# Second-layer keys kept on the chip, two weight buffers in the front, a first selection that begins with single heads

## The reference, cut to what matters

```python
sh1, sc1, g1, sh2, sc2, g2 = split(silu(c) @ ada_w[l] + ada_b[l])
x = x + g1 * mixer(rms_norm(x) * (1 + sc1) + sh1)
x = x + g2 * peer_ffn(rms_norm(x) * (1 + sc2) + sh2)

def peer_ffn(h):                                  # per block of 128 tokens
    q = (h @ wq).reshape(n, 8, 2, 128)            # 8 heads, two sides
    s = einsum('nhpd,hpkd->nhpk', q, keys)        # 128 keys for each head and side
    v1, i1 = top_k(s[:, :, 0], 16); v2, i2 = top_k(s[:, :, 1], 16)
    top_s, pos = top_k(v1[..., :, None] + v2[..., None, :], 16)   # of 256 pairs
    idx = i1 * 128 + i2 at pos; g = softmax(top_s)
    act = gelu(einsum('nhkd,nd->nhk', w_down[idx], h))
    return einsum('nhk,nhkd->nd', g * act, w_up[idx])
```

## Time and profile before

| | |
|---|---|
| Median of 3 runs | 3246.12 us (3245.19 to 3246.56) |
| The profiled execution | 3249.22 us, span 3247.4 us, mean granted TensorE clock 0.80 |
| Busy | TensorE 2348.6 us (72%), VectorE 2212.8 (68%), ScalarE 1281.3 (39%), GpSimd 1205.5 (37%) |
| Moved | 1288.67 MB, mean 397 GB/s |
| Of it by GpSimd's queue (q0) | 1124.14 MB; by SyncE's (q1) 162.07 MB |
| The chain that ended last | DMA 33%, TensorE 32%, VectorE 20%, ScalarE 8% |

### The profile page before, as it was taken

How to read it: one execution, slowest core, us unless ns; L and a number is a source line. 1 busy time by engine, 2 the same in 40 slices (tenths; PEclk the granted TensorE clock), 3 DMA queues, 4 the chain that set the end, 5 groups by cost and what they waited for, 6 DMA issues and landing times.

```text
span 3247.4 us, 38543 instructions
## 1 busy us (share of the span) xinstructions
PE 2348.6 (72%) x13032; PEld 923.5 (28%) x13032; DVE 2212.8 (68%) x5634; ACT 1281.3 (39%) x3704; POOL 1205.5 (37%) x1076
## 2 busy tenths in 40 slices
PE   6997678576776778786695696956686667856666
PEld 2345234122341235441151261511143112511110
DVE  2314875876569555869858968589948996795444
ACT  2212453345534453533433534333343433443333
POOL 1112243343434342334433434334433453343332
PEclk9998889687887888886696896967687777866676
DMA  8777999999999999999999999999999999999998
GB/s 321 262 284 288 400 377 423 420 395 408 416 422 409 417 398 422 397 422 408 421 402 420 408 413 420 391 403 398 420 398 421 405 421 403 422 398 421 421 420 357
DMA packets 170486, 1288.67 MB, mean 397 GB/s; under 512 B 19632, under 2 KB 20528, under 8 KB 24112
## 3 DMA queue, kind: packets, MB, share of 16 engines
q0 software_dynamic: 154368, 1124.14, 84.9%
q1 hardware_dynamic: 15920, 162.07, 12.0%
HBM read 1284.04 MB, written 2.10 MB: 396 GB/s over the span
## 4 chain that ended last, share of the span: by engine, by line
DMA 33%; PE 32%; DVE 20%; ACT 8%; issue 7%; POOL 1%; DVEq 0%; ACTq 0%; SPq 0%; POOLq 0%
DMA ring<-in_experts,expert 31%; PE psum L1792 10%; DVE ring L1495 8%; PE psum L1559 7%; PE psum L1573 5%; PE psum L1739 3%; DVE arena L1382 3%; PE psum L1531 1%; PE psum L1590 1%; ACT shares_of L1119 1%; ACT diag L1120 1%; PE psum L1545 1%; DVE arena L1410 1%; ACT acts L1118 1%; ACT L1118 1%
## 5 line engine op out<-in xcount | busy, mean ns | idle before, releaser
L1792 PE MATMUL psum<-ring,diag 64*64 64x512 f32 x8192 | 1415.1, 796 | 766.1 <-ACT diag L1120 760.7
L843 POOL DMA_INDIRECT ring<-in_experts,expert x1024 | 1179.8, 1152 | 1791.2 <-PE psum L1792 1654.3
L1495 DVE CUSTOM_DVE_ANT_0 ring<-ring,h 128x1024 f32<-128x1024 f32 x1024 | 1230.8, 1223 | 528.7 <-DMA ring<-in_experts,expert 506.5
L1118 ACT ACTIVATE acts<-dots 128x1 f32<-128x1 f32 x1024 | 206.5, 202 | 1475.2 <-DVE dots L1495 1439.2
L1792 PEld LDWEIGHTS psum<-ring,diag 64*64 64x64 f32 x8192 | 284.1, 161 | 1726.3 <-ACT diag L1120 1536.8
L1120 ACT ACTIVATE diag<-ident_half,shares_of 128x64 f32<-128x64 f32 x1024 | 356.1, 348 | 33.3
L1119 ACT ACTIVATE shares_of<-acts,gate 128x1 f32<-128x1 f32 x1024 | 301.7, 295 | 33.3
L1382 DVE SCALAR_TENSOR_TENSOR arena<-kept,taps,arena 128x128 f32<-128x128 f32 x960 | 262.6, 346 | 0.1
L1573 PEld LDWEIGHTS psum<-arena,weights 128*128 128x128 f32 x1984 | 226.8, 192 | 49.2 <-issue 45.4
L1573 PE MATMUL psum<-arena,weights 128*128 128x128 f32 x1984 | 238.1, 278 | 0.4 <-DMA weights<-in_chunks 0.4
L869 ACT ACTIVATE arena<-psum 128x512 f32<-128x512 f32 (+1 forms) x105 | 65.5, 624 | 219.3 <-PE psum L1573 121.9
(11 more groups left out here) (170 smaller groups left out, 1605.9 us busy)
## 6 DMA issues: line engine op xcount, KB each, us to landing
weights<-in_chunks SPq DMA_DIRECT2D x67, 2048.0 KB
ring<-in_chunks POOLq DMA_DIRECT2D x46, 1024.0 KB, 5.7
ring<-in_experts,expert POOLq DMA_INDIRECT x1024
arena<-in_chunks SPq DMA_DIRECT2D x16, 512.0 KB
ring<-in_chunks SPq DMA_DIRECT2D x3, 2048.0 KB, 8.9
x<-in_x SPq DMA_DIRECT2D x1, 2048.0 KB, 14.0
kept<-in_chunks POOLq DMA_DIRECT2D x2, 1024.0 KB, 18.2
out_x<-x SPq DMA_DIRECT2D x4, 512.0 KB
```

The source lines that it names most:

```text
L843: pool.indirect_dma_start(out=ring[:, k, :], out_offset=None, in_=table, in_offset=bass.IndirectOffsetOnAxis(ap=expert[:, s.b % 2, n:n + 1 ...
L1118: step(act.activation(acts[:, k:k + 1], dots[:, k:k + 1], ACT.Gelu))
L1495: dve.tensor_tensor_reduce(out=ring[:, k, 0:D], in0=ring[:, k, 0:D], in1=h2[:, s.b % 2, :], scale=1.0, scalar=0.0, op0=ALU.mult, op1=ALU.a ...
L1792: pe.matmul(ffn_out[rows_out, r * COLS:(r + 1) * COLS], diag[rows_in, k, :], ring[rows_in, k, D + n * COLS:D + (n + 1) * COLS], start=Fals ...
```

## The change

1. `SIDE` names five buffers instead of three, and the third weight buffer is gone: the chunks of the front have two. GpSimd no longer waits for the last chunk in it.
2. From unit 1 on GpSimd waits for `side_landed[1]` instead of `x_landed`. SyncE's wait for `side_landed[5]` and the first chunk now stand ahead of the eleven small parameter loads.
3. In `FRONT` the values' first phase v0 stands behind w1, t1 and w2 instead of ahead of w1.
4. Selection takes its heads in pieces: `PIECES` as before, `FIRST_PIECES` for block 0 of layer 0, where the first two pieces are one head each. GpSimd may then fetch 16 slots at first, 16 more after the second piece, then 32 each. `SELECT_WITH_EVEN` and `EVEN_LEFT` are written anew for the 28 phases, with 0.7 in place of `SHARED` (0.6).
5. ScalarE's exponential comes ahead of the evacuation of the same phase.
6. The keys' second half in layer 1 has a place of its own (`kept[:, 5120:6144]`). In layer 1 block 0 loads both halves, block 1 the first half only, and blocks 2 and 3 none.

```diff
+PIECES = [(0, 2), (2, 4), (4, 6), (6, 8)]
+FIRST_PIECES = [(0, 1), (1, 2), (2, 4), (4, 6), (6, 8)]
...
-    SIDE = (8, 0, 1)
+    SIDE = (8, 0, 1, 2, 3)
...
-                open_to = range(self.BUFS + (last[c] < gathers[0]))
-                c.buf = min(open_to, key=lambda b: last[held[b]] if held[b] else -1)
+                c.buf = min(range(self.BUFS), key=lambda b: last[held[b]] if held[b] else -1)
...
-        s = Stage("select", layer=layer, b=b, first=first, cost=(1.3,) * (3 if first else 5) + (2.5,) * (5 * QUARTERS))
+        s = Stage("select", layer=layer, b=b, first=first, cost=(1.3,) * (3 if first else 5) + tuple(
+            1.4 if hi - lo == 1 else 2.5 for lo, hi in (FIRST_PIECES if first else PIECES) for _ in range(5)))
...
+            if layer and b > 1 - half:
+                s.keys.append(self.kept_keys[half])
+            else:
+                new.append(self.key((layer * 2048 + half * 1024, layer * 2048 + (half + 1) * 1024),
+                                    s.s[1] if half and not layer else ("ht_ready", s.ht), layer * half))
+                s.keys.append(new[-1])
...
 SELECT_WITH_EVEN = """
-s8 s9 s10 s11 n0 s12 n1 s13 n2 q0 s14 q1 g0 s15 q2 g1 s16 q3 q4 s17 g2 g3 q5 s18 a0 a1 s19 a2 a3 g4 s20 a4 a5 s21 a6 a7 s22
+s8 s9 s10 s11 s12 n0 s13 n1 s14 n2 q0 s15 q1 g0 s16 q2 s17 g1 q3 q4 s18 g2 g3 s19 q5 a0 s20 a1 a2 s21 a3 g4 s22 a4 a5 s23 a6 s24 a7
+s25 a8 a9 s26 a10 a11 s27
 """
...
-q0 u11 q1 t0 k12 w0 v0 w1 t1 q2 q3 q4 v1 w2 r0 q5 a0 w3 a1 ...
+q0 u11 q1 t0 k12 w0 w1 t1 w2 v0 q2 q3 q4 v1 r0 q5 a0 w3 a1 ...
...
-        stages = mixer(1, 3)
-        return alone(p.gate_row(0, G2)) + written(stages | {"s": select}, SELECT_WITH_EVEN, SHARED) + written(stages, EVEN_LEFT)
+        stages = mixer(1, 1)
+        return alone(p.gate_row(0, G2)) + written(stages | {"s": select}, SELECT_WITH_EVEN, 0.7) + written(stages, EVEN_LEFT)
...
-        key_half = at(3072, 1024)
+        keys_at = [at(3072, 1024), kept[:, 5120:6144]]
...
             sp.dma_start(x[:], A["x"].rearrange("(t p) n -> p t n", p=P)).then_inc(x_landed, 16)
+            sp.wait_ge(side_landed[5], 16)
+            load_chunk(0)
             sp.dma_start(iota16[:], A["iota16"]).then_inc(params, 16)
...
-            sp.wait_ge(side_landed[5], 16)
-            for n in range(len(plan.chunks)):
+            for n in range(1, len(plan.chunks)):
                 load_chunk(n)
...
-                    pool.wait_ge(x_landed, 32)
+                    pool.wait_ge(side_landed[1], 16)
...
-            t, part = plan.last_extra.last_use
-            pool.wait_ge(full[t.bank], t.full_after[part])
...
-                    if n % (SLOTS_PER_BLOCK // QUARTERS) == 0:
-                        pool.wait_ge(S["topk_ready"], QUARTERS * s.index + QUARTERS * n // SLOTS_PER_BLOCK + 1)
+                    if n // TOPK in [lo for lo, hi in pieces] and n % TOPK == 0:
+                        chosen_before += 1
+                        pool.wait_ge(S["topk_ready"], chosen_before)
...
-                for n in range(s.lists + 5 * QUARTERS):
+                for n in range(len(s.cost)):
+                    if n >= s.lists and (n - s.lists) % 5 == 4:
+                        exponent((n - s.lists) // 5)
                     what, q, part = s.work[n] if n < len(s.work) else ("wait", 0, 0)
...
-                    if n >= s.lists and (n - s.lists) % 5 == 4:
-                        exponent((n - s.lists) // 5)
                     yield
...
-                for q in range(QUARTERS):
-                    dve.wait_ge(S["scores_ready"], s.sc + q + 1)
-                    lists, heads = range(4 * q, 4 * q + 4), range(2 * q, 2 * q + 2)
+                for i, (lo, hi) in enumerate(s.pieces):
+                    dve.wait_ge(S["scores_ready"], s.sc + lo // 2 + 1)
+                    lists, heads = range(2 * lo, 2 * hi), range(lo, hi)
...
```

More of the change, by code:

```diff
@@ L128, in __init__ @@
         self.turned = None
-        self.keys_loaded = 0
+        self.keys_loaded, self.kept_keys = [0, 0], []
     def tile(self, parts=1):
@@ L135, in chunk, with key @@
         return Chunk(source, cols)
-    def key(self, cols, after):
-        return Chunk(KEY_CH, cols, after)
+    def key(self, cols, after, place):
+        c = Chunk(KEY_CH, cols, after)
+        c.place = place
+        return c
     def place(self):
@@ L153, in place @@
                 last[c] = at
-        gathers = [at for at, (s, phase) in enumerate(self.order) if s.kind == "gather"]
-        held, landed = [None] * (self.BUFS + 1), [0] * (self.BUFS + 1)
+        held, landed = [None] * self.BUFS, [0] * self.BUFS
         for at, (s, phase) in enumerate(self.order):
@@ L373, in select @@
         s.q, s.s = [self.tile() for _ in range(QUARTERS)], [self.tile() for _ in range(QUARTERS)]
-        s.keys = [self.key((layer * 2048 + half * 1024, layer * 2048 + (half + 1) * 1024), s.s[1] if half else ("ht_ready", s.ht))
-                  for half in range(2)]
+        s.keys, new = [], []
+        for half in range(2):
+            if layer and b > 1 - half:
[4 more added lines that the diff above has]
+                s.keys.append(new[-1])
+        self.kept_keys = s.keys
         s.work = SELECT_FIRST if first else SELECT
@@ L383, in select @@
                 s.claim(phase, s.s[q])
-                if q % 2 == 0:
+                if q % 2 == 0 and s.keys[q // 2] in new:
                     s.read(s.keys[q // 2], phase, phase, s.s[q + 1], 0)
@@ L650, in trunk_kernel @@
         ctx_x = store[:, 6144:8192].rearrange("p (t n) -> p t n", t=CTX // P)
-        def eight(held):
-            return held.rearrange("p (k n) -> p k n", k=KD)
-        buffers = [weights[:, i] for i in range(Plan.BUFS)] + [eight(store[:, 12288:16384])]
+        buffers = [weights[:, i] for i in range(Plan.BUFS)]
         side_bufs = [held[:, i * 2048:(i + 1) * 2048].rearrange("p (k n) -> p k n", k=KD // 2)
@@ new lines, in combine @@
+                def combine(i, lo, hi):
+                    slots, part = slice(TOPK * lo, TOPK * hi), part_f(lo, hi)
+                    step(dve.scalar_tensor_tensor(out=part[:, 0, :], in0=part[:, 0, :], scalar=float(N_KEYS), in1=part[:, 1, :],
+                                                  op0=ALU.mult, op1=ALU.add))
+                    issue(dve.tensor_scalar(expert[:, s.b % 2, slots], part[:, 0, :], float(s.layer * N_EXPERTS), None, ALU.add))
+                    dve.wait_ge(S["gate_exp"], s.exp + i + 1)
+                    step(dve.tensor_reduce(gate_sum[:, lo:hi], best_v[:, lo:hi, :], AX.X, ALU.add))
+                    step(dve.reciprocal(gate_sum[:, lo:hi], gate_sum[:, lo:hi]))
+                    issue(dve.tensor_tensor(gate[:, s.b % 2, slots].rearrange("p (h n) -> p h n", h=hi - lo), best_v[:, lo:hi, :],
+                                            gate_sum[:, lo:hi, None].to_broadcast([P, hi - lo, TOPK]), ALU.mult))
```

123 lines of the change are left out of this document (57 added, 66 removed).

## The result

The changed kernel took 3226.74 us (median of 4 runs, 3218.3 to 3228.01) beside 3246.34 us (4 runs, 3245.19 to 3248.34) for the kernel before on the same chip: ratio 0.9935, 95% interval 0.9919 to 0.995, 19.6 us less. Forecast: 3229, range 3216 to 3240. The profiled execution took 3228.01 us, span 3226.1, so the two traces differ by 21.3 us of span. In what follows "sooner" means: than the same instruction in the trace of before.

What follows compares the result with a forecast made beforehand. TensorE bounds the front, waits 215 to 260 us, VectorE 340 to 463, then full DMA at 421 GB/s. Gains 1.3 + 6.7 + 3 + 0 + 2 + 0 + 5 = 18.0, less 1: 17; 3249.2 - 17 - 3.1 gives 3229 us, range 3216 to 3240.

Steps and rivals of the forecast that it cites:

- Rival (b): Sooner stream passes whole (7.1 us), keys give 6.2, x harmed little (4): 27 us in all, 3219 us; chance 0.18.
- (a): Key loads covered by TensorE, second head eats the sooner start: only the front's 10 to 11 us, 3236; chance 0.20.
- (c): x starved, chain at 215 us waits as long for ScalarE and VectorE: 3.4 us gained, 3243; chance 0.07.
- (d): Slower: the front's weight loads wait for a buffer, 6.7 us per late one; four give 3256 us; chance 0.05.
- Part 1: Start: first weight halves no longer wait for x, mod ready at 44.4 instead of 45.15; gain 1.3 us, bounds +7, -4.
- The -4 end: Lower bound of the start's gain: x slowed by the halves lands only at 29 us, losing 4 us.
- All three 0: Start: later parameters, the query chunk behind them, and half 8 onward each cost 0 us.
- Part 2: Front after 200 us: five halves remove two late-half waits; gains 6.7 us before the output projection, 3 before the norm's transposes.
- Part 3: Front: two weight buffers instead of three, V's chunk just in time at 123 for 125.2; 0 us, bounds 0 and -7.
- Part 4: First selection: single heads and earlier exponential, first fetch 7.1 us sooner, but only 2 us gained; bounds -4 and 7.
- Part 5: Second layer's keys: five 512 KB loads fewer, 6.2 us where the DMA is full; gain 5 us, bounds 0 and 6.2.
- What would show it: Trace signs: mod near 44, no late halves after 200 us, first fetch near 274, five key loads missing.

Runs made afterwards that it cites:

- three key runs: Kernel before with kept keys alone, 3237.97 us; changed kernel with all sixteen key halves loaded, 3231.93 us; kernel before with eight key halves loaded twice, 3252.61 us.
- two halves earlier: Changed kernel with modulation halves 4 and 5 ahead of the second three of x's transposes in TensorE's order: 3226.05 us.
- exponential last: Changed kernel with ScalarE's exponential behind the evacuation again, single heads kept: 3228.55 us.
- pairs: Changed kernel with the first selection in pairs of heads, old phase order and share 0.6, the exponential still ahead: 3227.27 us.
- three halves: Changed kernel with three weight halves in rotation again instead of five: 3235.02 us.

## Why the prediction was right, point by point

**The sum.** 17 us were forecast; the traces differ by 21.3, the medians by 19.6, 19.1 and 21.1. Rival (b) has 27, and the medians lie between the two, nearer the forecast: its keys came true (6.0 and 7.0 for 6.2), but the sooner stream did not pass whole (3.5 us of 7.3 at the first product). (a) is refuted by the three key runs; (c) and (d) by the trace after: no half late, no chunk waited for at V. That the total is so close is in part luck. Up to the first product the trace has 17.8 us where the sum had 12, and the keys gave 1 or 2 more than their 5; that makes 24 to 25, where the medians show 19 to 21. Some 4 us that the sum put at nothing are lost in the stream or belong to the scatter of the traces. Two pieces of the change, v0's new place and the third weight buffer, were not undone by themselves; the trace shows only that no wait hangs on either.

**Part 1: mod 2.9 us sooner for 1.3, and not by one edit alone.** x came at 22.88 where I had taken 24. DMA queues of the changed kernel from 10 to 13 us, then from 14 to 20 (packets, MB, share of the engines; x is in q1):

```profile
q1 hardware_dynamic: 325, 1.27, 103.3%
...
q0 software_dynamic: 211, 1.60, 64.2%
q1 hardware_dynamic: 221, 0.90, 37.4%
```

The halves are issued at 9.89, but none of their data moves before 13.6: x has the engines to itself for more than 3 us. Then it gets 36% of the bytes, not far from the 30% of the forecast. So in the bound of 29 ("at 30% from 9.5 us on") the start was wrong, not the share; that x has the queues to itself for a while, the reason for taking 24, was right. The 30% was lucky all the same. The earlier trace rows is an average of unlike stretches: from 5 to 8 us SyncE's queue moved 0.05 MB in 180 small packets, from 9 to 10 it had the engines alone (102 packets, 0.41 MB, beside one). In the changed kernel from 14 to 20 us, where both queues move, there are 211 packets to 221 as the profile counts them, against 208 to 373 in the earlier trace rows, and the bytes went by the size of a packet there, 7.6 KB (1.60 MB in 211) to 4.1 (0.90 in 221). The -4 end did not come.

From x to mod I counted 20.4; it was 19.4 (transposes 9.0 us behind x, as counted, 4.8 to the first of the four halves instead of 4.6, four halves 3.6, turning and adding 1.9 where I allowed 3). There was a slip too: 45.15 - 44.4 is 0.75, and the sum carried 1.3. Measured: 2.9. The cause I gave, halves that no longer wait for x, is enough for it (41.98 with the parameters first) but not needed (42.25 with the old wait and the parameters moved). "All three 0" was right for the parameters only because half 5 landed early: SyncE issued K at 27.23, with the parameters behind it; with the old wait they came late and cost VectorE 2 us and TensorE 3.46.

**Part 2, right.** 6.7 forecast, 6.5 measured at the output projection (10.5 less the 4.0 by which 210.17 was already sooner); 3 forecast, 2.9 at the transposes. Undoing it cost 9.5 to 11.5 us at the end for 9.7, and 7.6 at the first fetch.

**Left out: the clock's part of the front.** 14.3 us at the first WQ matmul are 2.9 + 1.1 + 6.5 + 2.9 + 0.9, where the sum had 1.3 + 6.7 + 3 - 1. Of the 1.1, 0.7 are K's first tile (5.58 us, 6.29 before); the 0.9 is the norm's first tile of transposes at 1.09 instead of 1.97. Both are the granted clock: 0.58 before and 0.66 after in K's tile, 0.50 (256.5 to 258.5 us) and 1.00 (243.1 to 244.3) in the other. The run with two halves earlier lost such tiles again, and the kernel before with kept keys had K's first tile at 5.58 too, so they seem to hang on the timing of a run rather than on the edit.

**Part 3, right at 0.** K was read at 107.31, not 110.93, V was needed at 121.20, not 125.2: 13.9 us for the 12 I counted, and no wait. The 1 us held back for it was not needed.

**Part 4, first fetch right, remainder small as forecast.** 7.1 us forecast, 7.3 measured (21.6 - 14.3). Of it 3.5 were left at the first product (17.8 - 14.3) where I took 2. The loss came sooner than I put it. From the first fetch to its product the queues carried weight chunks and rows:

```profile
q1 hardware_dynamic: 228, 3.47, 67.1%
q0 software_dynamic: 228, 1.74, 33.9%
```

In the same stretch before, these were 1.20 MB of chunks and 1.80 of rows. The sooner rows met chunks that used to go out ahead of them. Other traces bear it out: 8.4 us from issue to use with 1.23 MB of chunks (exponential last), 9.5 with 2.00 (pairs), 11.9 with 3.31 (three halves). "In the old gap the DMA was not empty" was the right reason; its size was guessed. What the second head and the weave cost behind that isn't settled: by slot 512 the three traces keep 15.6, 19.8 and 20.1 us of lead for the same code.

**Part 5, right, on the low side.** 5 forecast (0 to 6.2); 6.0 and 7.0 by medians, +2.0 to +7.6 in the leads of ten traces, 5.5 in the mean. Full DMA (share 1.01, 421 to 424 GB/s from 2400 to 2460 us) decided, not TensorE's 54 of 60 us.

**What would show it** held in kind: no half late after 200 us, no wait at V, five key loads less, and none of the signs of being wrong. The sizes were mostly too small: mod at 42.24 for 44, the output projection 10.5 us sooner for 8, the norm's transposes 13.4 for 11, the first fetch at 270.06 for 274, the lead at slot 128 17.7 for 12. By the medians a key load gave 1.2 to 1.4 us for about 1.

## What to carry to other kernels

Where the trace has the DMA full, price a load that goes by its bytes over the rate there (here 1.25 us for a key half at 421 GB/s, 1.0 to 1.4 measured), whatever the other engines' busy share says; where it is not full, look for the wait that it ends. When two queues share, split the window until the shares stay the same: here SyncE's queue had 30% of the bytes from 5 to 10 us, but the engines alone from 9 to 10, and 36% from 14 to 20 in the changed kernel. A buffer that ends two waits is worth the waits plus what the matmuls behind them lose at the lower clock (here 3.37 and 3.86 us of waiting, and 1.94 instead of 1.07 us for a half), and it also made this front repeat from run to run (first fetch at 268.70 to 270.06 in four traces, 286.49 to 293.65 in three with the late halves). A microsecond won at the start can be gone at the first fetch: with mod 2.2 us sooner the fetch left 0.35 us later, behind tiles at a lower granted clock (transposes 1.97 us at 0.50, 1.09 at 1.00). Read the duration of the same tile at several places before counting it.

## What the runs showed of the hardware that I had not expected

- In two stretches of the changed kernel's trace where both queues had large transfers, their packets came one to one and the bytes by the size of a packet: 211 to 221 packets from 14 to 20 us, 1.60 MB of halves to 0.90 of x; 60 to 61 from 279 to 282.3, 0.48 MB of expert rows to 1.00 of chunks. Against rows SyncE's chunks got two thirds there, against halves its x got one third (36%).
- In the changed kernel data of a load on GpSimd's queue first moved some 4 us after the issue (halves issued at 9.89, first data at 13.6; first row issued at 270.06, data from 274). Until then the other queue had the engines to itself (1.27 MB, share 103.3%, from 10 to 13 us; 1.70 MB, 102.8%, from 270.06 to 274).
- An instruction on SyncE that only issues a small load took 6.72 us (conv_par at 39.84, halves still landing) where it took 0.43 in the changed kernel; that load was what VectorE waited for.
- The first fetched row took 12.2 us from issue to use with 3.47 MB of chunks on the other queue, 8.5 us with 1.20 MB.
- A tile of eight transposes took 1.97 us or 1.09 by small shifts of time: the norm's first 1.97 at 256.55 before and 1.09 at 243.16 after, its second 1.09 at 245.99 after and 1.97 at 244.72 with mod 2.2 us sooner. The granted clock of 245 to 250 us was 0.74 in that last kernel and 1.00 in the changed kernel again.
